# Two-layer hybrid trunk on eight cores: the gate projection of the second pass reads unnormalised h, the first loads are issued in order of use, and the rope table is stored once

## The reference

```python
def rmsnorm(x, g):                       # over the last axis, in float32
    return x * rsqrt(mean(x*x) + 1e-6) * g
cos, sin = rope_tables(positions, 64)
for i in range(2):                       # DEPTH
    z = rmsnorm(h, norm_mix[i]) @ w_in[i]            # 1024 -> 3008 columns
    q_a, k_a, v_a, gate_a, c_q, c_kv, k_rope, gate_b = split(z)
    o_a = chunked_relpos_attention(q_a, k_a, v_a, rel_bias[i])   # 8 heads, band of 576 keys
    o_b = mla_attention(c_q, c_kv, k_rope, ..., cos, sin)        # 4 heads, block-causal
    h = h + concat(o_a * silu(gate_a), o_b * silu(gate_b)) @ w_out[i]
    gate = sigmoid(rmsnorm(h, norm_ple[i]) @ w_pg[i] + b_pg[i])
    h = h + (p[i] @ w_pe[i]) * gate
return rmsnorm(h, norm_final)
```

## Time and profile before

| | |
|---|---|
| median of 3 runs | 2501.28 us (2499.81 to 2699.69) |
| the profiled execution | 2502.74 us |
| its span, slowest core | 2501.2 us (cores: 2490.4 to 2501.2) |
| mean granted TensorE clock | 0.967 |
| PE busy | 2157.4 us, 86% |
| DVE busy | 1256.6 us, 50% |
| ACT busy | 1213.6 us, 49% |
| POOL busy | 180.5 us, 7% |

### The profile page before, as it was taken

How to read it: one execution, slowest core, us unless ns; L and a number is a source line. 1 busy time by engine, 2 the same in 40 slices (tenths; PEclk the granted TensorE clock), 3 DMA queues, 4 the chain that set the end, 5 groups by cost and what they waited for, 6 DMA issues and landing times.

```text
span 2501.2 us, 46758 instructions; the slowest of 8 cores (2490.4 to 2501.2 us)
## 1 busy us (share of the span) xinstructions
PE 2157.4 (86%) x14928; PEld 1091.7 (44%) x14928; DVE 1256.6 (50%) x2623; ACT 1213.6 (49%) x2222; POOL 180.5 (7%) x509
## 2 busy tenths in 40 slices
PE   0288999899989999999979889999989999978895
PEld 0144545454444444444434344445434445434343
DVE  1355535435564443566655555362655533465665
ACT  1334748484465575444324364555535658433342
POOL 1200000000010110000020000000000000000000
PEclk9999999999999999999988999999999999999998
DMA  9613203120322482655331101010110115163442
GB/s 173 172 35 93 79 16 83 36 59 20 85 52 43 85 169 70 180 157 153 94 96 47 45 29 35 26 39 22 52 43 27 26 35 119 59 156 95 127 116 68
DMA packets 99331, 194.97 MB, mean 78 GB/s; under 512 B 11800, under 2 KB 28696, under 8 KB 96280
## 3 DMA queue, kind: packets, MB, share of 16 engines
q1 hardware_dynamic: 90168, 164.19, 22.6%
q0 software_dynamic: 8928, 27.79, 7.0%
HBM read 165.19 MB, written 54.53 MB: 88 GB/s over the span
## 4 chain that ended last, share of the span: by engine, by line
PE 73%; DVE 10%; issue 5%; DMA 5%; ACT 4%; POOL 1%; SPq 1%; DVEq 0%; ACTq 0%; POOLq 0%
PE psa L349 69%; PE psa L353 3%; ACT sb_pt L361 2%; DMA sb_mx<-pos 2%; PE psa L357 1%; POOL sb_rcs L367 1%; DVE sb_pt L380 1%; DVE sb_mx L380 1%; DVE sb_sc L367 1%; DMA sb_sc<-mixd 1%; DVE sb_sc L380 1%; SPq L394 1%; DVE sb_qb L367 1%; DVE sb_qa L380 1%; DVE sb_sg L380 1%
## 5 line engine op out<-in xcount | busy, mean ns | idle before, releaser
L361 ACT ACTIVATE sb_pt<-psa 128x512 bf16<-128x512 f32 x1248 | 656.1, 549 | 206.0 <-PE psa L349 178.3
L349 PE MATMUL psa<-sb_hb,sb_w 128*128 128x512 bf16 x2560 | 654.8, 386 | 35.7 <-DVE sb_sg L380 29.6
L349 PEld LDWEIGHTS psa<-sb_hb,sb_w 128*128 128x128 bf16 x2560 | 241.6, 99 | 286.9 <-issue 76.6
L349 PE MATMUL psa<-sb_qb,sb_ckt 128*128 128x512 bf16 (+3 forms) x1280 | 341.1, 347 | 4.7 <-ACT sb_pt L361 2.0
L349 PE MATMUL psa<-sb_ckvt,sb_pt 128*128 128x129 bf16 x2176 | 236.3, 220 | 5.3 <-POOL sb_pt L390 2.3
L349 PE MATMUL psa<-sb_qa,sb_ka 128*128 128x384 bf16 (+3 forms) x896 | 221.7, 301 | 15.5 <-ACT sb_pt L361 10.8
L367 DVE TENSOR_TENSOR sb_pt<-sb_pt,sb_eb 128x256 bf16<-128x256 bf16 (+2 forms) x608 | 172.2, 295 | 92.5 <-ACT sb_pt L361 86.7
L349 PEld LDWEIGHTS psa<-sb_ckvt,sb_pt 128*128 128x128 bf16 x2176 | 164.5, 97 | 123.6 <-issue 17.5
L349 PEld LDWEIGHTS psa<-sb_va,sb_pt 128*128 128x128 bf16 x2240 | 122.9, 98 | 118.7 <-issue 96.9
L349 PE MATMUL psa<-sb_va,sb_pt 128*128 128x65 bf16 x2240 | 160.5, 195 | 15.0 <-DVE sb_pt L367 6.6
L387 DVE RECIPROCAL sb_rcp<-psa 128x4 f32<-128x4 f32 (+1 forms) x256 | 44.8, 175 | 244.2 <-PE psa L349 239.3
(11 more groups left out here) (131 smaller groups left out, 2556.0 us busy)
## 6 DMA issues: line engine op xcount, KB each, us to landing
sb_xs<-x SPq DMA_DIRECT2D x116, 256.0 KB, 4.0
mixd<-sb_mx SPq DMA_DIRECT2D x128, 128.0 KB, 2.1
sb_xs<-h SPq DMA_DIRECT2D x56, 256.0 KB, 3.3
sb_w<-w_in POOLq DMA_DIRECT2D x24, 512.0 KB, 11.8
sb_cs<-ropes SPq DMA_DIRECT2D x16, 512.0 KB, 3.4
sb_sc<-mixd SPq DMA_DIRECT2D x8, 1024.0 KB, 6.3
sb_qb<-mixd SPq DMA_DIRECT2D x8, 1024.0 KB, 5.4
sb_hb<-w_out POOLq DMA_DIRECT2D x8, 512.0 KB, 6.4
```

The source lines that it names most:

```text
L349: S.op("pe", lambda h: h.matmul(out, lhsT=lhsT, rhs=rhs, start=start, stop=stop, skip_group_check=skip), reads=reads, writes=writes, inc=l ...
L361: S.op("act", lambda h: h.activation(out=out, in_=in_, func=func, **kw), reads=reads, writes=writes, cost=c)
```

## The change

In the second pass `hb2` becomes h times the gain alone, made by ACT (a Copy with a scale) while `OP` runs, with a buffer of its own for odd groups in `CKT`. The gate matmuls read it. The row factor, spread in `rbp`, is applied by DVE to their product in PSUM, and Tanh reads the result from SBUF. The streams are P (both `OP` and `PLE`), G (sums and factor of `OP`) and F (sums, final scaling). Four PSUM banks rotate instead of two for `OP` and two for the gate, and the small product has two banks.

At the start, the position load is issued first, the first weight pair next, and the other weight transfers wait until chunk 5 of x(0) has landed. x(1) waits for the tenth weight pair, the bias table for the eighth. The costs of the planner change: weight bandwidth from 110 to 220, SP's from 160 to 170, ACT's fixed part from 0.19 to 0.17. The rope table is written once (96 rows, 3 stores a group) and read back by two DMAs that repeat rows: cos with four copies, the sines with two. `S1` moves two gates ahead of the spreading of its row factors and `T_KR` directly behind it. `x_load` of layer 1 waits for less in group 0, and the bias table is staged in `SG` in two halves.

```diff
-                    wire[e] = max(wire.get(e, 0.0), end) + o.size / (160e3 if e == "sp" else 110e3)
+                    wire[e] = max(wire.get(e, 0.0), end) + o.size / (170e3 if e == "sp" else 220e3)
@@ ACT
-        c = 0.19 + fsize(out) * 0.000833 + ...
+        c = 0.17 + fsize(out) * 0.000833 + ...
@@ load_w1
+            gate = hb_r[1][2:4] if l == 0 else []
-                dma(W1[:, a:a + 2, :], w_in_d[l, :, a:a + 2, :], [], W1_r[a:a + 2], f"d_w1_{a}", eng="pool")
+                dma(W1[:, a:a + 2, :], w_in_d[l, :, a:a + 2, :], gate if i else [], W1_r[a:a + 2],
+                    f"d_w1_{a}", eng="pool")
@@ prep_e
-            tp = CKT[:, 1:5, :].rearrange("p a b -> p (a b)").bitcast(F32)
+            tp = SG[:, 4096:6144].bitcast(F32)
+            for g in range(2):
+                dma(tp, extb_d[l]...[:, g * 1024:(g + 1) * 1024],
+                    [W1_r[T_KA + 2]] if l == 0 else [], sg_r[2], "d_ext")
@@ prep_rope
-                    for r in range(4):
-                        dma(rope_d[n, r * 32:(r + 1) * 32, 0, :], tab[rows, 512:1024], ...)
-                        dma(rope_d[n, r * 32:(r + 1) * 32, 1, :], neg[rows, :] if r % 2 == 0 else tab[rows, 0:512], ...)
+                    for r, src, rg in ((0, tab[rows, 512:1024], R3), (1, neg[rows, :], R0), (2, tab[rows, 0:512], R3)):
+                        dma(rope_d[n, r * 32:(r + 1) * 32, :], src, rg, [rope_dr[n][r]], f"d_rpo{k}_{r}")
@@ x_norm
-                S.need("hb_0_0")
+                S.need("hb_0_0", "W0")
-                        dma(xa, x_d[s, t, :, c, :], [], xr, ...)
+                        dma(xa, x_d[s, t, :, c, :], [W1_r[T_QA + 2]] if n == 1 else [], xr, ...)
@@ x_load
-                S.need(f"OP_{l - 1}_7", f"Q_{l - 1}_{n * 7}")     # and Qm_{l-1}_7 for n == 0
+            if n == 0:
+                S.need(f"OP_{l - 1}_7", f"Q_{l - 1}_0")
+                nst, rb, xb = 3, 1, 7
@@ S1
-            dma(CS[:, :, :], rope_d[n], rope_dr[n], [cs_r], "d_cs")
+            dma(CS[:, 0, :], bass.AP(rope_d.tensor, rope_d[n, 0:1, 0:1].offset, [[0, 4], [SL, 32], [1, SL]]), ...)
+            dma(CS[:, 1, :], bass.AP(rope_d.tensor, rope_d[n, 32:33, 0:1].offset, [[0, 2], [SL, 64], [1, SL]]), ...)
             gate(T_GB + 1, 1 + b, 1)
+            gate(T_GB + 2, 1 + b, 2)
+            gate(T_GB + 3, 1 + b, 3)
             ... both spreadings of the row factors, then zmm(T_KR) and its four DVE operations, then the scalings
@@ OP
+                bk = (PB if n == 0 else R4).next()
                 TT(hch(b, fc), PS[bk], hch(b, fc), ALU.add, ...)
+                ACT(hb2(b, fc), hch(b, fc), AF.Copy, ..., scale=gple[:, l, fc:fc + 1])
+                square(l, n, "g", fc, SQ1, sq_r, hch(b, fc), hall(b, fc))
+            S.at("G")
+            col_sums(l, n, "g", SQ1, sq_r, 7)
+            k = rstd_tail(4, PS[7], PR[7], ((4, 1.0 / DM),))
+            bcast(rcs[:, k, 0:4], rcs_r[k], 4, 7)
+            ACT(rbp(b), PS[7], AF.Copy, [PR[7]], rbp_r[b])
@@ PLE
-            for c in range(8):
-                STT(hb2(c), hch(b, c), gple[:, l, c:c + 1], RB[:, 0, :], ALU.mult, ALU.mult, ...)
             for fc in range(8):
-                by = PGB.next()
+                by = R4.next()
-                ACT(utf(ui), PS[by], AF.Tanh, ..., bias=hbpg[:, l, fc:fc + 1], scale=0.5)
+                TT(t_, PS[by], rbp(b), ALU.mult, ...)
+                ACT(t_, t_, AF.Tanh, ..., bias=hbpg[:, l, fc:fc + 1], scale=0.5)
+                if fc >= 1:
+                    fin(fc - 1)
+            fin(7)
+            S.at("F")
+            col_sums(l, n, "f", SQ2, onb_r, 6)
@@ order of the parts
-        load_w1(0, ())
         prep_rope()
-        prep_e(0, ("hb_0_1",))
+        load_w1(0, ())
+        prep_e(0, ("W0",))
-        S.merge(["T", "Q", "P", "X", "L", "R", "W", "V", "Z", "E"], {"T": 1, "Q": 2, "P": 3})
+        S.merge(["T", "P", "G", "F", "X", "L", "R", "W", "V", "Z", "E"], {"T": 1, "P": 2})
```

212 lines of the change are left out of this document (105 added, 107 removed).

## The result

The changed kernel takes 0.9672 of the time of the one before, interval 0.9614 to 0.9729: about 2420 us (two runs gave 2420.0 and 2423.6) against 2501. Faster by 82 us (68 to 97 by the interval); 144 was forecast.

What follows compares the result with a forecast made beforehand. PE was taken as the bound except at the start, the seam and layer 1's second pass, where a chain bounds. Gains of 64 + 60 + 10 + 10 = 144 us from 2502.7 gave a forecast of 2358 us, range 2320 to 2408.

Steps and rivals of the forecast that it cites:

- 85 - 21 = 64 us gained: Start: first projections 85 us earlier, less 21 us for the rope-table stall, 64 us gained (45 to 85).
- The second position load, issued after the first stores, is as slow and falls into the same stall.: Start: the second sequence's position load adds no cost beyond the 21 us stall for the rope table.
- badly ordered start: Rival, start: a late transfer early in an engine's fixed order leaves only 30 us gained, 2392 us; chance 0.09.
- the forecast's 33: Start: the first projection matmul of S1(0) comes near 33 us, not 118.
- The rope-table stall of 21 us: First group: narrow table reads beside the weights land near 71 us, needed at 50; cost 21 us, between 0 and 35.
- x_norm(1) ... is ready well before S1(0) ends: Start: normalising group 1's x starts on the tenth weight pair, near 50 us, and is ready before group 0's projections end.
- I take nothing, with 8 us either way: Rest of S1 and the planner's other costs: reordering counted as no gain, with 8 us either way.
- Layer 1's second pass: Second pass of layer 1: 281 us against 341, 60 us gained (40 to 72).
- Layer 0's with the seam: Layer 0's second pass 10 us (0 to 17) and the seam between the layers 10 us (5 to 14) gained.
- four banks carry it: Second pass: the row factor is needed only when a product must leave PSUM, for which four banks give 6.9 us.
- VectorE-bound: Rival, second pass: DVE's order becomes the bound, 39 us or more a group in both layers, about 2410 us; chance 0.14.
- narrow-reads-on-every-group: Rival, first passes: narrow table reads hold up x and h1 loads in every group, 2640 us; chance 0.02.

Runs made afterwards that it cites:

- late_pos: The changed kernel with the load of the second sequence's positions held until the last pair of first-layer weights has landed; 2390.7 and 2394.1 us.
- direct: early_pos with group 0's rope tables copied straight from the buffer they are computed in, and two small weights moved out of their place; 0.9513, 2376 us.
- after_act: The changed kernel with the planner's fixed cost of a ScalarE instruction back at 0.19 us instead of 0.17; 0.9552, 2383 to 2389 us.
- after_s1: The changed kernel with the first pass's order of instructions of the kernel before; 0.9622, 2400 to 2406 us.
- best_act: direct_s1x with the planner's fixed cost of a ScalarE instruction at 0.19 us instead of 0.17; 0.9413, 2349 and 2354 us.
- two_banks: The changed kernel with its second pass's products in turn through two PSUM banks instead of four; 2453.3 and 2460.3 us.
- direct_s1x: direct with the first pass's order of instructions of the kernel before and earlier loads of x for group 1; 0.9478, 2366 us.
- early_cs: early_pos with each rope-table read cut into pieces of 32 or 64 whole rows, all six on semaphores of their own; 0.9528, 2379 us.
- early_pos: The changed kernel with both position loads ahead of the x loads, with own buffers for them and for the second sequence's table; 0.9566, 2390 us.

## Why the prediction was wrong

**The step that failed is the start's sum, "85 - 21 = 64 us gained", at the sentence "The second position load, issued after the first stores, is as slow and falls into the same stall."** The load is that slow (23.5 us, not far from the 19.6 taken from the earlier trace rows). But it falls into no other stall: it makes its own, ahead of the eight scalings, where I had only put the first load and x. I had costed what must land before S1(0), and not asked what stands ahead of S1(0)'s inputs in VectorE's order; the rival "badly ordered start" names this mechanism and has 30 us gained at mark 1, where 35.4 were measured, though its time of 2392 missed as well. The sign was in the trace of before: that load was waited for there, for 10.08 us, ahead of the same copies. late_pos shows it: the chain elsewhere, mark 1 is 41.4 and 28 us come back. The 8 us that are left to the forecast's 33 are a sum too short: the spread factor was to be there at 27.6 and the scalings began at 35.1, and the gated weights started at 24.2 instead of 18 and were in at 68 instead of 58. The rope-table stall of 21 us exists too; it is covered in the changed kernel by the longer one, and measured 13.0 and 15.8 us where that was taken away. With it gone (direct) another 14 us came back. "x_norm(1) ... is ready well before S1(0) ends" failed by the same neglect of a queue: x went out at 122.6, behind stores and exponentials. "The planner can put the memsets in the idle time before 18 us" failed as well, without cost: POOL ran them from 36.7 to 49.5, before anything read them.

**The second step that failed is "I take nothing, with 8 us either way"** for the rest of S1 and the planner's costs. One of these costs measured 30 us (after_act), the order of the first pass 15.0 in layer 0 less 10.6 in layer 1, 12 by the ratios (after_s1). With the start they come to nearly 70 us (best_act) where 62 were missing; the edits don't add, so the sum can't be shared out among them. That the planner's number acts by the order alone is shown (nothing else differs), and in layer 1 the order acts through the waits for the rope products, 13 of 14 us. Between marks 2 and 3 the new order of the first pass costs its 15 us in two ways: TensorE is busy 653.7 us instead of 644.5 for as many matmuls, at a granted clock of 0.977 instead of 0.984, and its waits are 56 us instead of 52 (medians).

**What held.** Layer 1's second pass, 62.3 us against 60 (60.3 by the medians), and for the reason given: `sb_sc` gone from the waits, the clock at 1.00. Layer 0's with the seam, 19.8 against 20; layer 1's projections start at 1243.14, right behind the last products of PLE(7) at 1242.28. That four banks carry it (two_banks) was a clause of the argument, and is worth over half of the term. VectorE-bound and narrow-reads-on-every-group did not happen: in later groups the table reads hide.

**What stays open.** From mark 1 to mark 2 even direct_s1x needs 158 us, before needed 146 with two groups' x already normalised. After mark 1 no single wait of TensorE up to 140 us is over 2 us, and the granted clock is 0.83 from 70 to 80; no run separates what is left. Why the old order lowers the clock in layer 1 and raises it in layer 0 was not settled either.

## What to carry to other kernels

When loads are moved to the front, write down for each engine in fixed order what is queued ahead of the first useful instruction and which transfer each of these waits for: one chain of a later stage, waiting for one 256 KB load, held the first group back by 41 us. A plan made with a cost table is one draw among many: change a constant by its last digit, run, and keep the best, before a gain or loss is put down to the edit beside it. Price a transfer by the row that has the same company, not the same size. Read a length off several cores before giving it a cause: one core alone made 14 us look like 20 here, and 6 like nothing.

## What was not expected of the hardware

- Small transfers from SP's queue beside the weights that POOL's queue brings in and casts: 64 to 128 KB pieces issued from 40 us took 17.4 to 23.1 us to land, and 1.9 to 2.8 when alone (early_cs). The wait grows the later they are issued into that stream: in the same run 64 KB stores took 6.2 us (median) when issued from 25 to 30 us, and 12.6 and 15.6 from 35 to 40. So the 8.2 to 11.1 us of the copies within on-chip memory (direct) don't show that such a copy is quicker by itself: they were issued from 33 to 38, and stores to device memory issued from 30 to 35 and from 35 to 40 took 6.5 and 12.4 in that run. What the copy saves is the second transfer.
- TensorE's granted clock, in a stretch of 10 us in which it did nothing in the middle of work, was 0.50, and 0.55 in the next 10 us (early_pos, above), the lower level of 1.2 GHz. The matmuls behind the stall of 47 us ahead of the work ran at the lower pace as well, though the column doesn't say so. Windows of the changed kernel, core 2:

```profile
82.83:87.90 5.07, 5.07 (x12) 1.72 (x13) 2.83 (x6) 1.31 (x3) 0.00 (x0) 1.00 0.00 0
88.00:92.00 4.00, 4.00 (x20) 1.82 (x19) 1.12 (x2) 2.35 (x4) 0.00 (x0) 1.00 0.32 83
```

The same matmuls take 0.42 us each in the first stretch and 0.20 in the second, and both read 1.00. The kernel before starts alike: nine in 3.60 us from 118.2, then twenty in 4.00. Where the column and the length of the matmuls disagree, go by the length.
